# Feed-forward up products with the weights stationary and 256 tokens moving, in a two-block mixer kernel

## The reference

```
h = rmsnorm(x, ln2_g[layer])
u = h @ w_up                          # 2048 -> 2 * 5632
up = pad(u, one token on each side)
u = sum(up[:, i:i + t] * conv_w[i] for i in range(3)) + conv_b
a, g = split(u, 2, axis=-1)
x = x + (a * silu(g)) @ w_down        # 5632 -> 2048
```

## Time and profile before

| | us |
|---|---|
| median of 3 runs | 3719.89 (3716.03 to 3721.61) |
| profiled execution, its own time | 3718.52 |
| its span in the profile | 3716.7 |
| PE busy | 3534.9, 95% of the span |
| DVE busy | 2319.8, 62% |
| ACT busy | 1863.5, 50% |

### The profile page before, as it was taken

The page is one execution under the profiler, slowest core; times in us unless marked ns, Lnnn a source line. Parts: engine busy times, 40 slices in busy tenths (PEclk is TensorE's granted clock), DMA queues, the critical chain, the costliest instruction groups (busy, mean ns, idle before and its releaser), DMA issues.

```text
span 3716.7 us, 43000 instructions
## 1 busy us (share of the span) xinstructions
PE 3534.9 (95%) x16794; PEld 2854.4 (77%) x16794; DVE 2319.8 (62%) x3204; ACT 1863.5 (50%) x2544; POOL 54.5 (1%) x101
## 2 busy tenths in 40 slices
PE   7899889999889999999999999999999999999998
PEld 5688668779758776778788788787777888878876
DVE  5487466578465556656666666656665566666665
ACT  4634545543645436555444444453556554444444
POOL 3000000000000000000000000000000000000000
PEclk9999999999999999999999999999999999999999
DMA  7333436433436435455565565563444655555554
GB/s 216 116 108 103 130 98 193 140 109 103 120 96 205 133 103 146 141 166 181 181 189 179 178 191 182 176 195 97 135 141 143 198 182 182 181 186 180 179 188 150
DMA packets 398524, 577.70 MB, mean 155 GB/s; under 512 B 25186, under 2 KB 222298, under 8 KB 397681
## 3 DMA queue, kind: packets, MB, share of 16 engines
q1 hardware_dynamic: 392544, 557.93, 49.3%
q0 software_dynamic: 5328, 15.83, 1.4%
q10 hardware_dynamic: 448, 1.18, 0.1%
HBM read 570.65 MB, written 4.19 MB: 155 GB/s over the span
## 4 chain that ended last, share of the span: by engine, by line
PE 79%; DVE 11%; ACT 7%; issue 2%; DMA 1%; DVEq 0%; ACTq 0%; SPq 0%
PE PS L699 76%; DVE WL L1802 3%; PE PS L696 3%; ACT WH L1283 2%; DVE AR L1942 1%; DVE AR L2448 1%; DVE AR L2443 1%; DVE X L1812 1%; ACT L1544 0%; DMA RAW<-in_w_in 0%; DVE AR L2455 0%; DVE AR L2268 0%; DVE AR L2453 0%; ACT AR L1613 0%; DVE SM L2207 0%
## 5 line engine op out<-in xcount | busy, mean ns | idle before, releaser
L1802 DVE TENSOR_TENSOR WL<-RAW,WH 128x1024 fp32r<-128x1024 f32 x1056 | 1286.7, 1223 | 1004.0 <-ACT WH L1283 1003.5
L1283 ACT ACTIVATE WH<-RAW 128x1024 fp32r<-128x1024 f32 x1056 | 1105.5, 1055 | 1001.3 <-PE PS L699 987.4
L699 PE MATMUL PS<-WH,Ah 128*128 128x512 f32 x3520 | 1426.1, 405 | 62.2 <-DVE WL L1802 34.9
L699 PE MATMUL PS<-WL,Ah 128*128 128x512 f32 x3520 | 1380.7, 392 | 0.0
L699 PE MATMUL PS<-WH,Al 128*128 128x512 f32 x3520 | 1379.3, 392 | 0.0
L699 PEld LDWEIGHTS PS<-WH,Ah 128*128 128x128 f32 x3520 | 666.1, 189 | 239.4 <-issue 51.3
L699 PEld LDWEIGHTS PS<-WL,Ah 128*128 128x128 f32 x3520 | 665.4, 189 | 144.1
L699 PEld LDWEIGHTS PS<-WH,Al 128*128 128x128 f32 x3520 | 667.0, 189 | 134.3 <-issue 5.3
L699 PE MATMUL PS<-AR 128*128 128x128 f32 (+5 forms) x2208 | 312.6, 294 | 19.5 <-DVE GT L2225 7.1
L699 PEld LDWEIGHTS PS<-AR 128*128 128x128 f32 (+3 forms) x2208 | 266.0, 192 | 72.0 <-PE PS L699 25.8
L699 PE MATMUL PS<-WH,Zh 128*128 128x512 f32 x704 | 280.3, 398 | 27.1 <-DVE WL L1802 27.1
(11 more groups left out here) (312 smaller groups left out, 2108.4 us busy)
## 6 DMA issues: line engine op xcount, KB each, us to landing
RAW<-in_w_in SPq DMA_DIRECT2D x368, 512.0 KB, 3.7
RAW<-in_w_up SPq DMA_DIRECT2D x704, 256.0 KB, 3.1
RAW<-in_w_down SPq DMA_DIRECT2D x176, 512.0 KB, 4.6
RAW<-in_w_out SPq DMA_DIRECT2D x64, 512.0 KB, 3.7
RAW<-in_w_o SPq DMA_DIRECT2D x64, 512.0 KB, 3.9
RAW<-in_w_in SPq DMA_DIRECT2D x64, 256.0 KB, 3.0
AR<-in_c POOLq DMA_DIRECT2D x2, 1600.0 KB, 8.9
AR<-bias_scratch POOLq DMA_DIRECT2D x16, 192.0 KB, 4.6
```

The lines of the kernel that those rows point to most:

```text
L699: return T.matmul(o, lhs, rhs, start=start, stop=stop, skip_group_check=True)
L1283: act(WH[:, j % NW, 0:n], raw_view(j), ACT.Copy).then_inc(*w_hi())
L1802: tt(WL[:, j % NW, 0:w], raw_view(j), WH[:, j % NW, 0:w].bitcast(F32), SUB).then_inc(*w_lo())
```

## The change

In the up chunks the operands of the matmul change places. A 128 x 128 piece of the weights is now stationary and the 256 tokens move, so the sums come out with channels on partitions and need no transposes. A slice takes 12 matmuls of 256 columns instead of 6 of 512. The 1/rms now has to be a row, the same on all partitions: once for each layer, PE multiplies `RSTD`, spread over 128 columns, with the identity, and DVE copies the result to `RROW`. ACT's scaling goes; DVE multiplies the sums of a chunk by the row into `UT` in one instruction (step `xs`), which also frees the banks. The three taps read `UT` instead of PS. The a's and b's of DVE get a `yield` between them, and the steps of all three engines take one pump more.

```
@@ tile of PE
+                    if ch.phase == "up":
+                        for i in R4:
+                            o, at = ptile(s, i), slice(128 * i, 128 * i + 128)
+                            mm(o, wh[:, k, at], hi[:, kk, :], beg and i % 2 == 0, False)
+                            mm(o, wh[:, k, at], lo[:, kk, :], False, False)
+                            ins = mm(o, wl[:, k, at], hi[:, kk, :], False, end)
+                        continue
@@ prepare of PE, after the turns of quarter c
+                if c == 3 and r in (3, 5):
+                    T.wait_ge(*p_rs.at(2 * r + 1))
+                    T.wait_ge(*p_gt.at(gt_index(r, 2, 1)))
+                    for t in R2:
+                        ins = mm(PS[:, 4, 128 * t:128 * t + 128], RSTD[:, t:t + 1].broadcast_to([128, 128]), ident)
+                    ins.then_inc(*w_pe(str((r - 3) // 2)))
                 yield
@@ leave_up of PE
-                yield
-                T.wait_ge(*f_act.at(f"{l}.{c}.sc1"))
-                if c >= 2:
-                    T.wait_ge(*f_dve.at(f"{l}.{c - 2}.b3"))
-                for i in R4:
-                    for t in R2:
-                        o = 256 * (i % 2) + 128 * t
-                        ins = tr(PS[:, 4 + 2 * u + i // 2, o:o + 128], UT[u][:, t, 128 * i:128 * i + 128])
-                ins.then_inc(*f_pe(f"{l}.{c}.tr"))
-                yield
-                yield
+                for _ in range(4):
+                    yield
@@ leave_up of ACT
-                if c >= 2:
-                    A.wait_ge(*f_pe.at(f"{l}.{c - 2}.tr"))
-                scaled(UT[u], ch, f_act, [k + ".sc0", k + ".sc1"])
-                yield
-                yield
-                A.wait_ge(*f_pe.at(k + ".tr"))
+                yield
+                A.wait_ge(*f_dve.at(k + ".xs"))
...
-                    act(CV[u][:, i, :], PS[:, 4 + 2 * u + i // 2, 256 * (i % 2):256 * (i % 2) + 256], ACT.Identity,
+                    act(CV[u][:, i, :], UT[u][:, i, :], ACT.Identity,
                         bias=P(("fcb", l), q), scale=P(("fcw", l), 88 + q)).then_inc(*f_act(f"{k}.ct{i}"))
+                yield
+                yield
                 yield
                 A.wait_ge(*f_dve.at(k + ".b3"))
@@ prepare of DVE
+                if c == 3 and r in (3, 5):
+                    V.wait_ge(*w_pe.at(str((r - 3) // 2)))
+                    cp(RROW, bank(4, 256)).then_inc(*w_dve(str((r - 3) // 2)))
@@ leave_up of DVE
+                V.wait_ge(*w_used.at(ch.end))
+                V.wait_ge(*w_dve.at(str(l)))
+                if c >= 2:
+                    V.wait_ge(*f_dve.at(f"{l}.{c - 2}.b3"))
+                ps = PS[:, 2 * (ch.index % 2):2 * (ch.index % 2) + 2, :].rearrange("p b (i n) -> p (b i) n", n=256)
+                tt(UT[u], ps, RROW.unsqueeze(1).broadcast_to([128, 4, 256]), MUL).then_inc(*f_dve(k + ".xs"))
                 yield
                 yield
...
-                    stt(CV[u][:, i, 1:256], ps[:, 0:255], P(("fcw", l), q), CV[u][:, i, 1:256],
+                    stt(CV[u][:, i, 1:256], UT[u][:, i, 0:255], P(("fcw", l), q), CV[u][:, i, 1:256],
                         MUL, ADD).then_inc(*f_dve(f"{k}.a{i}"))
+                yield
```

More of the change, by code:

```diff
@@ L496, in program @@
         ups = range(22)
-        f_act = steps("up_act", [f"{l}.{c}.{n}" for l in LL for c in ups for n in ("sc0", "sc1", "ct0", "ct1", "ct2", "ct3", "th", "hi")])
-        f_pe = steps("up_pe", [f"{l}.{c}.tr" for l in LL for c in ups])
+        f_act = steps("up_act", [f"{l}.{c}.{n}" for l in LL for c in ups for n in ("ct0", "ct1", "ct2", "ct3", "th", "hi")])
+        w_pe, w_dve = steps("row_pe", ["0", "1"]), steps("row_dve", ["0", "1"])
         f_dve = steps("up_dve", [f"{l}.{c}.{n}" for l in LL for c in ups
-                                 for n in ("a0", "a1", "a2", "a3", "b0", "b1", "b2", "b3", "th", "zz", "lo")])
+                                 for n in ("xs", "a0", "a1", "a2", "a3", "b0", "b1", "b2", "b3", "th", "zz", "lo")])
         QW, KW, SK, ALG, DTB, LAMP, RDL = [], [], [], [], [], [], []
@@ L621, in program @@
         TH = [ar(8192, 2, 256), ar(8704, 2, 256)]
-        UT = [ar(9216, 2, 512), ar(10240, 2, 512)]
+        UT, RROW = [ar(9216, 4, 256), ar(10240, 4, 256)], ar(11264, 256)
         FG, XN = ar(4096, D), ar(0, 2, D)
@@ L640, in set_free @@
             if ch.phase == "up":
-                return f_act.at(f"{l}.{n}.sc1")
+                return f_dve.at(f"{l}.{n}.xs")
             if n in ("ba", "ga"):
@@ L1248, in leave_up @@
             def leave_up(ch):
-                l, c, u = ch.l, ch.name, ch.name % 2
-                yield
-                T.wait_ge(*f_act.at(f"{l}.{c}.sc1"))
-                if c >= 2:
-                    T.wait_ge(*f_dve.at(f"{l}.{c - 2}.b3"))
-                for i in R4:
-                    for t in R2:
-                        o = 256 * (i % 2) + 128 * t
-                        ins = tr(PS[:, 4 + 2 * u + i // 2, o:o + 128], UT[u][:, t, 128 * i:128 * i + 128])
-                ins.then_inc(*f_pe(f"{l}.{c}.tr"))
-                yield
-                yield
-                e.flags.add(f"z{c}")
+                for _ in range(4):
+                    yield
+                e.flags.add(f"z{ch.name}")
             def close():
@@ L2441, in leave_up @@
                 for i, q in enumerate(cols):
-                    ps = PS[:, 4 + 2 * u + i // 2, 256 * (i % 2):256 * (i % 2) + 256]
-                    stt(CV[u][:, i, 1:256], ps[:, 0:255], P(("fcw", l), q), CV[u][:, i, 1:256],
+                    stt(CV[u][:, i, 1:256], UT[u][:, i, 0:255], P(("fcw", l), q), CV[u][:, i, 1:256],
                         MUL, ADD).then_inc(*f_dve(f"{k}.a{i}"))
+                yield
                 for i, q in enumerate(cols):
-                    ps = PS[:, 4 + 2 * u + i // 2, 256 * (i % 2):256 * (i % 2) + 256]
                     V.wait_ge(*f_dve.at(f"{k}.a{i}"))
-                    stt(CV[u][:, i, 0:255], ps[:, 1:256], P(("fcw", l), 176 + q), CV[u][:, i, 0:255],
+                    stt(CV[u][:, i, 0:255], UT[u][:, i, 1:256], P(("fcw", l), 176 + q), CV[u][:, i, 0:255],
                         MUL, ADD).then_inc(*f_dve(f"{k}.b{i}"))
```

## The result

The changed kernel takes 3727.67 us in the median of 11 runs (3727.12 to 3730.15), the kernel before 3719.89 in as many of the same sessions. The ratio is 1.0023, 95% interval 1.0015 to 1.0031: slower by 8 us, or 0.2%. The forecast was 3671, so 57 us are missing, and the sign is wrong.

What follows compares the result with a forecast made beforehand. PE was taken to set the time, though not alone, losing time to transposes and waits. Transposes -40.7, products +0, waits -40.4 + 29.0 and row +3.0 made -49.1, so 3671 us by the median; range 3652 to 3705.

Steps and rivals of the forecast that it cites:

- the products: Up chunks on PE: 4224 matmuls of 512 columns become 8448 of 256, at 0.1133 us per pair: +0.
- The range: Forecast span for the whole kernel, 3652 to 3705 us, leaving out slower rivals, no change and the short chain.
- the loss of the single precision pairs: Upper bound for the products: 0.0046 us lost beside 0.1067, laid on 0.1133, gives 0.118 per pair, +39 us.
- A pair at 120: Rival for the up matmuls: a full load's price makes the pair 120 ns, +57 us, to 3728; chance 0.06.
- The break-even: Up matmuls: from 119.1 ns per pair on, 5.8 ns more than taken, the change loses.
- Transposes, waits and row together: All PE terms but the products: transposes -40.7, waits -40.4 + 29.0, row +3.0; sum -49.1 us.
- The chain through the down part: Down part, first addition to late tile: grows from 9.74 to 12.0 us, PE losing 1.45 per group, 29.0 in all.
- No cover left ahead of it: Ahead of the down part's chain: side work ends at 5.6 us, first addition may start at 5.64.
- The row of 1/rms: PE behind a layer's second tile: waits 0.9 us for the exponential, then four passes; 1.5, twice, 3.0 us.
- Instructions too slow: Rival on PE's up matmuls: instructions come too slowly, 125 ns a pair, +99 us, to 3770; chance 0.06.
- loads bare: Rival on PE's up matmuls: 4224 added weight loads not hidden, 0.11 each, +465 us, to 4136; chance 0.01.
- DVE the bound: Rival: DVE's order becomes the bound, `xs` standing wholly in the chain, +24 us, to 3695; no separate chance given.

Runs made afterwards that it cites:

- the kernel with 512 moving columns: The changed kernel with its up matmuls put back to 6 of 512 moving columns per slice, all else as changed: 3672.06 us, ratio 0.9871 against the kernel before.
- order alone: The kernel before with only the change's order: a pump between DVE's a's and b's, last step one pump later; transposes and ACT's scaling stay: 3708.49 us, ratio 0.9969.

## Why the prediction was wrong

The step that failed is **the products**, and in it one sentence: "So the time goes by the moving columns, whatever was loaded." The pair takes 120 ns and not 113.3: +0 in my sum, +56 on the chip.

- *What the rows allowed.* The earlier trace rows and the 0.2267 of today's tiles fit two readings. By one the time is 0.443 ns for each moving column; by the other each pair has a price on top of its columns at 2.4 GHz, 6.6 ns with 32 stationary columns, 13.4 with 128. Both were in the prediction. I took the first, since 12 and 32 stationary columns cost the same, and gave the second 0.06. It said 120 ns and 3728 us; measured were 120 and 3727.67. That its number came true does not make its rule true: 512 moving columns with 32 stationary ones lose 18 ns and not 6.6. The first reading would have asked 0.127 for 288 columns and 0.142 for 320; they took 0.132 and 0.147.
- *Why misled.* They show a full load each 0.111 us, and that was right (0.112 for 192 and 224 moving columns). I took it as a floor under which the matmul hides, so that the larger of 0.111 and 0.1133 counts. But at 256 columns the pair takes 0.120, above both, so load and matmul do not hide each other there as a floor would have it.
- *The range.* Its upper end came from the loss of the single precision pairs, 0.0046, laid on the new pair. That term gave +39, 3710, and the range ends at 3705, short of even that, without a reason. A pair at 120 was written down among the rivals, yet the range left it out. The 13.4 ns were the loss of the same type with the same load, a nearer row than another type's.
- *The break-even* was right: 119.1 ns. 120 is 0.9 ns beyond it, 8 us.

The other steps, each by its own measurement:

- *Transposes, waits and row together:* -49.1 forecast, -48.1 measured in the kernel with 512 moving columns (-43 to -53 by its interval). The 40.7 for the transposes goes by 1.85 us for two; 44 x 0.93 would be 40.9.
- *The chain through the down part:* the wait moved one tile down, 12.15 us of chain for 12.0 and 1.54 us lost for 1.45, and order alone gave 11.7 us for 11.
- *No cover left ahead of it:* the down part starts at 2262.51 and the first addition at 2268.18, 5.67 us for the forecast 5.64.
- *The row of 1/rms:* 1.36 us per layer for 1.5.
- *Instructions too slow, loads bare, DVE the bound:* none of them. PE takes 384 pairs in a row at 120 ns, where bare loads (0.11 more) would make them some 220; bfloat16 pairs of 128 columns come every 56 ns; DVE is busy 46.08 of 69.43 us.

What stays open is what the price of a pair is made of. With a full load it is 12 to 14 ns from 256 to 384 columns and at 512, some 16 at 448 and 480 (0.203 and 0.217 per pair); with a small load it grows with the moving columns; in turn 512 and 256 pay 33 ns for two. I found no rule for all of these, and did not need one for the verdict: the very pair of the kernel was measured in the changed kernel, in the kernel before with that orientation alone, and by itself.

## What to carry to other kernels

Swapping the operands leaves the moving columns as they are but not the number of pairs, and in this type each pair has a price on top of its columns. Here halving the moving width cost 6% of the up matmuls, more than the transposes it saved. If two readings of a trace differ by a few nanoseconds that are taken thousands of times, the sum must carry both to the range, with the break-even beside them. And look at the order first: the kernel before had more to gain from `yield`s put elsewhere (38 us) than from a new layout.

## What the hardware showed that I had not expected

- fp32r pairs with a full load lose 13.3 ns each at 256 moving columns, bfloat16 ones of the same shape 2.4 (0.109 per pair). The Trainium skill ("TensorE: Matmul & The Clock Gate", section "Back-to-back issue gap") gives the gap of a single matmul as its columns at the upper clock and 2.5 ns; the bfloat16 pairs agree with that, load and all, the fp32r pairs do not.
- With a full load, nothing is gained below 224 moving columns: 192 and 224 take 0.112 both.
- A wait of PE that cost 4.2 us by itself cost 7 in all, since the matmuls behind it ran at the lower clock (0.50 granted) for some 5 us.
